# Sixteen products of the identity with itself, at two waits of the modulation stage

## The reference

```
mod = silu(cond) @ w_mod[l] + b_mod[l]          # (2 conditions) x 6144; w_mod[l] is 2048 x 6144
shift, scale, gate = split(mod, 3)
xn  = rmsnorm(x) * (1 + scale) + shift
P   = xn @ w_in[l]                              # the front: queries, keys, values, gates, ...
A, B, C = attention(P), conv3(P), gla(P)        # three groups of heads
x   = x + gate * concat(A, B, C) @ w_out[l]
```

## Time and profile before

| | |
|---|---|
| median of 3 runs | 2180.7 us (2179.85 to 2181.5) |
| profiled execution | 2179.65 us, of which the span 2177.6 us |
| TensorE busy | 2137.2 us, 98% of the span |
| TensorE weight loads (beside the products) | 1891.6 us, 87% |
| VectorE, ScalarE, GpSimd busy | 1385.5, 650.7, 189.9 us |
| moved by the DMA engines | 364.17 MB, mean 167 GB/s |

### The profile page before, as it was taken

The page is one execution under the profiler, slowest core; times in us unless marked ns, Lnnn a source line. Parts: engine busy times, 40 slices in busy tenths (PEclk is TensorE's granted clock), DMA queues, the critical chain, the costliest instruction groups (busy, mean ns, idle before and its releaser), DMA issues. The chain is left out here.

```text
span 2177.6 us, 33774 instructions
## 1 busy us (share of the span) xinstructions
PE 2137.2 (98%) x13231; PEld 1891.6 (87%) x13231; DVE 1385.5 (64%) x2703; ACT 650.7 (30%) x1104; POOL 189.9 (9%) x125
## 2 busy tenths in 40 slices
PE   5999999999999999999999999999999999999998
PEld 3577887887899999999998888878789999999998
DVE  5469877986665666766367454455456666676654
ACT  4332121321333334443034212232123333343302
POOL 0000000000000000423321000000000000042331
PEclk9999999999999999999999999999999999999999
DMA  9999687664432324664445646444333233366444
GB/s 356 386 311 304 195 274 233 208 217 142 134 104 81 102 89 132 193 211 127 126 125 171 195 131 182 149 131 131 106 121 103 88 102 104 94 218 200 137 125 150
DMA packets 355312, 364.17 MB, mean 167 GB/s; under 512 B 17446, under 2 KB 261884, under 8 KB 354556
## 3 DMA queue, kind: packets, MB, share of 16 engines
q1 hardware_dynamic: 326224, 318.83, 47.0%
q10 hardware_dynamic: 28972, 43.74, 5.5%
HBM read 303.15 MB, written 59.38 MB: 166 GB/s over the span
## 5 line engine op out<-in xcount | busy, mean ns | idle before, releaser
L1709 DVE SCALAR_TENSOR_TENSOR macc<-mraw,cond,macc 128x384 f32<-128x384 f32 (+1 forms) x960 | 389.5, 479 | 0.0
L775 PE MATMUL psP<-x_high,high 128*128 128x512 f32 x896 | 357.8, 399 | 1.8 <-ACT stage L1247 1.0
L775 PE MATMUL psP<-x_high,low 128*128 128x512 f32 x896 | 349.7, 390 | 0.0
L775 PE MATMUL psP<-x_low,high 128*128 128x512 f32 x896 | 349.5, 390 | 0.0
L1228 ACT ACTIVATE high<-raw 128x1024 fp32r<-128x1024 f32 x128 | 135.5, 1058 | 511.5 <-PE psT L785 497.7
L810 PE MATMUL psP<-x_high,high 128*128 128x320 f32 x1024 | 242.7, 318 | 0.5 <-issue 0.5
L810 PE MATMUL psP<-x_high,low 128*128 128x320 f32 x1024 | 233.4, 309 | 0.0
L810 PE MATMUL psP<-x_low,high 128*128 128x320 f32 x1024 | 232.9, 309 | 0.0
L1727 DVE TENSOR_TENSOR low<-raw,high 128x1024 fp32r<-128x1024 f32 x128 | 163.8, 1280 | 89.1 <-ACT high L1228 89.1
L775 PEld LDWEIGHTS psP<-x_high,high 128*128 128x128 f32 x896 | 168.5, 188 | 53.0 <-issue 10.9
L775 PEld LDWEIGHTS psP<-x_high,low 128*128 128x128 f32 x896 | 168.5, 188 | 35.8
(11 more groups left out here) (318 smaller groups left out, 3627.0 us busy)
## 6 DMA issues: line engine op xcount, KB each, us to landing
raw<-in_w_in_dram SPq DMA_DIRECT2D x128, 512.0 KB, 5.1
wmod<-in_w_mod_dram SPq DMA_DIRECT2D x32, 1024.0 KB, 10.0
mraw<-in_w_mod_dram SPq DMA_DIRECT2D x64, 512.0 KB, 4.3
mraw<-in_w_mod_dram SPq DMA_DIRECT2D x32, 1024.0 KB, 7.2
raw<-in_w_in_dram SPq DMA_DIRECT2D x32, 1024.0 KB, 6.0
raw<-in_w_out_dram SPq DMA_DIRECT2D x64, 512.0 KB, 4.4
old<-x_scratch SPq DMA_DIRECT2D x64, 320.0 KB, 3.0
xf<-proj_scratch SPq DMA_DIRECT2D x48, 320.0 KB, 3.9
```

Source lines behind the costliest of these rows:

```text
L775: mm = pe.matmul(latent_ps[m], own, moved, start=(k == 0 and w is whole and x is x_high), stop=(k == KT - 1 and w is rest))
L1709: m = dve.scalar_tensor_tensor(acc[:, v, 0:width], mraw[hf][:, k, 0:width], c, acc[:, v, 0:width], ALU.mult, ALU.add)
```

## The change

Ahead of quarters 0 and 1 of block 2, eight products of the identity are put into TensorE's stream:

```diff
@@ -901,6 +901,8 @@
                     piece = 0
                     for t in range(2, MOD_CHUNKS):
                         for q in range(4):
+                            if t == 2 and q < 2:
+                                keep_busy(8)
                             mod_quarter(t, q)
                             if t % 2 == 1 and q == 0:
                                 mod_turn(t - 1)
```

## The result

The change makes the kernel a little slower. The median went from 2181.48 us to 2184.3 us (14 executions each); the ratio is 1.0014, with a 95% interval of 1.0007 to 1.0020. The forecast was 2180.7 us with a range up to 2183.4.

What follows compares the result with a forecast made beforehand. TensorE, 98% busy, was taken as the bound, nearly equalled by DMA until about 117 us. Span 2177.6 + 0, plus 2.05 for the whole execution and 1.05 to the median, gave 2180.7 us; range 2178.2 to 2183.4.

Steps and rivals of the forecast that it cites:

- The price of the products: Each group of eight added products at block 2 is 16 instructions at 0.117 us, 1.9 us; 3.2 at half pace.
- Both exposures: Product time not hidden in block 2's load waits: 0.5 us ahead of quarter 0, 0.7 ahead of quarter 1.
- The clock held: TensorE's granted clock stays 1.00 from 47 to 55 us, so 12 front products take 2.94 us, not 4.34.
- the front pieces still tied to VectorE's low half: After block 2's quarter 1, the first front piece cannot start before VectorE finishes its chunk's low half at 51.34 us.
- The lead lost at the loads: Block 2's quarters 2 and 3 start 1.4 and 1.3 us earlier; full DMA queues cancel this, gaining 0 by 116.78 us.
- The ceiling of 435 GB/s: Fabric limit at which this stage's loads would need some 61 us and the earlier start would be kept; forecast didn't use it.
- the rest of the trace is that of before: From block 3's quarter 3 at 67.97 us on, everything runs as before, with 0 gained at the last quarter, 116.78.
- 2177.6 + 0: The old span of 2177.6 us plus a net effect of 0 from the added products.
- rival C: Idle time moves to just ahead of 67.97 us and the clock falls there: +2.7 us, 2183.4; chance 0.05.
- A: Loads issued earlier land earlier, so the last quarter moves too: 1.3 us faster, 2179.4, at most 2178.2; chance 0.08.
- B: Products don't hold the clock at 47 us; the second eight cost 3.2 us: +0.9 us, 2181.6; chance 0.07.
- D: The change does not act: block 2's load ends the wait, clock recovers at 54 us; forecast time, sharing its 0.78.

Runs made afterwards that it cites:

- shift of 64: 64 more recorded TensorE instructions than the kernel before: the changed kernel (2184.2 us) or, without products, 128 already-met waits at the start (2185.3 and 2184.6 us).
- shift 160: Changed kernel plus 192 already-met waits in TensorE's start-up wait, 160 more recorded instructions than the kernel before: ratio 0.9995, mean 2180.3 us.
- shift 16: Kernel before plus 32 already-met waits at TensorE's start, 16 more recorded instructions, no products: 2180.6 and 2180.3 us.
- shift 32: 32 more recorded instructions than the kernel before: 64 already-met waits without products (2180.2 us), or only eight products ahead of block 2's quarter 0 (2181.6 us).
- first eight: Changed kernel with only the eight products ahead of quarter 0 of block 2, those ahead of quarter 1 removed: ratio 0.9994, mean 2181.6 us.
- wide products: Changed kernel with two 512-column identity products in place of eight 128-column ones at each of the two places: 2179.8 and 2179.7 us.

## Why the prediction was wrong

**What held.** The price of the products: 2.0 us for each group, where 1.9 was taken. Both exposures (quarter 0 at 47.46, forecast 47.45; quarter 1 at 50.41, forecast 50.3). The clock held; the front pieces still tied to VectorE's low half; quarter 2 at 54.34. The lead lost at the loads: the DMA share stayed at 1.05, the last quarter came at 116.48, 0.3 us early, where 0 +- 0.2 was given. The ceiling of 435 GB/s from the Trainium skill's page DMA: Bandwidth & Descriptors (section "Where 436 GB/s comes from") did not come into play; the loads stayed at 387 GB/s with the lead.

**The step that failed** is the sentence that "the rest of the trace is that of before", and the sum that follows from it, 2177.6 + 0. It treated the added instructions as time on TensorE only. They are also length in its instruction stream, and the page counts the fetches of that stream, q8, among the packets of the 16 DMA engines that move the data. The premise "What moves the last `wmod` product moves the end of the kernel one for one; what does not, moves nothing" fails with it: that product moved 0.3 us forward and the end 3.5 us back. At places far behind the change, where a load or a store is the last thing that TensorE waits for, the place of a fetch of 16 KB goes with about 0.5 to 1.7 us each. The shift of 64 hits several such places at once and costs 3.9 us (changed kernel against the same with shift 160: 2184.2 against 2180.3), up to 4.5 us without the products (2185.0 against 2180.5 at shift 16). Against the kernel before, timed beside it, the changed one costs 2.2 to 3.3 us in its four timings. I had the row in front of me, since the page lists the queue with its 78 packets, and I passed over it because its share is 0.2%. Waits of this kind stood in the profile of before too, the one on ScalarE's `stage` even in the earlier trace rows.

The range failed with the same step. It was built from the rivals' ends at one stage, where the largest price was 2.7 us, and so closed at 2183.4. The change measured, 2.8 us, is nearly that price, of rival C, but by luck: the cause is another. The rest of the distance is the base: the forecast starts from the median of three executions, 2180.7, and the median of 14 is 2181.5. The range left no room for this; the three executions span 1.7 us, the 14 span 4.7.

**The rivals.** A (lead kept) is not what the traces show; a rest of about 0.7 us is possible. B did not happen in any trace. C was described rightly at its place and is rare: one trace in nine with the clock held. Falls of the clock do add to the cost, but at 1023 us and later, behind waits that the prediction did not have. It isn't the cause of the slowdown, since the slowdown comes without products. D's first half was wrong: the change did act.

**What is shown and what is not.** Shown: the cost goes with a shift of 64 recorded instructions and not with the products, the clock at block 2 or the mere number of instructions; with it goes the longer wait at 370 us in all eight traces, and at two loads, the sin table of layer 0 and a tile of `w_out`, the delay follows the place of the fetch in all 18. Not shown: how the packet delays the load (a DMA engine taken from it is the obvious reading), and how the 3.9 us divide among the places. At 1019 us the waits at shift 32 (1.60 and 1.73) are as long as most at 64, with the fetch in that tile's flight in both, and yet these kernels are not slow; nor does a fetch in the sin load's flight by itself make one slow (first eight, 2181.6). No run moved a single fetch and left the others.

## What to carry to other kernels

An edit that adds instructions to TensorE's stream shifts its later instruction fetches, and in this kernel, whose loads land just in time, that alone was worth up to 0.2%, more than the edit itself. For the other engines no run shows it. Before a small change is judged, time a control that has the same number of added instructions and none of their work (waits that are already met, put in a long idle wait), and check the recorded count, since two waits were recorded as one instruction here. If the control is as slow as the change, move the fetches with a few more waits, or do the same work in fewer, wider instructions: here two products of 512 columns held the clock as well as eight of 128, at 2179.7 to 2179.8 us.

## What the runs showed that was not expected

- A packet of 16 KB on the instruction queue while the 256 KB sin table is loaded goes with a landing after 4.4 to 4.8 us in place of 3.0 to 3.2 if it starts about 2 us behind the issue. The Trainium skill's page Runtime: NRT & Kernel Launch (section "Instruction fetch mechanics") calls the cost of crossing such a block mostly hidden; for the fetching engine the traces agree (idle time put down to issue is 1.0 us before and after), but here the data loads come later.
- The second eight were not needed for the clock: with only the first eight products, and a wait of 1.09 us behind them, it stayed at 1.00 at block 2.
- The granted clock is written as 1.00 in the first transposes at 19.4 us of the kernel before, but they go at 0.20 us each. Transposes of the same size at the end of the kernel go at 0.22 us each where the clock is written as 0.50 (16 weight loads in 3.46 us) and at 0.11 where it is 1.00 (16 in 1.78). So the first ones ran near the half pace; the record of the clock begins only at 23.7 us.
- No version is clearly better than the kernel before. The wide products come nearest, with ratios of 0.9993 (0.9984 to 1.0002) and 0.9992 (0.9983 to 1.0001), but the kernel before against itself gave 0.9994.
